# Second and third modulation vectors: products with the weight rows on TensorE, or weighed running sums on VectorE

## The reference, cut to what matters

```python
silu_c, silu_cc = jax.nn.silu(c), jax.nn.silu(c_ctx)
for i in range(2):                                    # first_block
    need_ctx = i < 1
    mod_lat = (silu_c @ w_ada[i] + b_ada[i])[:, None, :]
    mod_ctx = silu_cc @ w_ada[i] + b_ada[i]
    sh_a, sc_a, g_a, sh_m, sc_m, g_m = jnp.split(mod_lat, 6, axis=-1)
    h_lat = x * (1.0 + sc_a) + sh_a                   # and h_ctx with mod_ctx
    ...                                               # attention
    x = layer_norm(alpha * x + g_a * y_lat, ...)
    x = layer_norm(alpha * x + g_m * sq_relu_mlp(x * (1.0 + sc_m) + sh_m, mlp_w1[i], mlp_w2[i]), ...)
    ...                                               # the same for xc, only if need_ctx
mod = silu(c_2) @ ada_w_2[0] + ada_b_2[0]             # second_block: six more parts, used in the same way
```

## Time and profile before

| | us |
|---|---|
| median of three runs (lowest, highest) | 2645.05 (2643.78, 2648.04) |
| the profiled execution: its own time | 2641.13 |
| its span, first to last instruction | 2639.3 |
| PE busy | 2513.5 (95%) |
| DVE busy | 1460.6 (55%) |
| ACT busy | 1037.6 (39%) |
| POOL busy | 720.9 (27%) |

### The profile page before, as it was taken

One profiled execution on the slowest core, in us unless ns is written; L12 is line 12 of the kernel. 1 busy time (PEld: TensorE's weight loads), 2 busy tenths in 40 slices (PEclk: granted clock), 3 DMA queues, 4 the chain that ended last, 5 costly groups with the idle time before them and its releaser, 6 DMA issues.

```text
span 2639.3 us, 39599 instructions
## 1 busy us (share of the span) xinstructions
PE 2513.5 (95%) x16734; PEld 1439.8 (55%) x16734; DVE 1460.6 (55%) x2251; ACT 1037.6 (39%) x1665; POOL 720.9 (27%) x967
## 2 busy tenths in 40 slices
PE   6999998999999998999999999989999999999999
PEld 3566655555555576467654444745644445844444
DVE  4469865663332226688764433279977775633341
ACT  3457743333221114577643322243353224533230
POOL 0210000527878762310022000015454562011100
PEclk8999999999999999999999999999999999999999
DMA  6520013555542221210035543232212333333340
GB/s 242 177 79 18 2 65 128 165 171 200 181 155 93 84 81 51 81 36 18 18 109 176 179 144 112 74 104 68 89 58 78 104 120 103 84 86 96 109 147 32
DMA packets 205616, 271.43 MB, mean 103 GB/s; under 512 B 10047, under 2 KB 181438, under 8 KB 196222
## 3 DMA queue, kind: packets, MB, share of 16 engines
q1 hardware_dynamic: 199054, 247.05, 29.1%
q0 software_dynamic: 5280, 18.64, 2.0%
q10 hardware_dynamic: 1104, 3.21, 0.3%
HBM read 252.62 MB, written 10.49 MB: 100 GB/s over the span
## 4 chain that ended last, share of the span: by engine, by line
PE 75%; DVE 13%; ACT 6%; DMA 3%; issue 2%; SPq 1%; POOL 1%; DVEq 0%; POOLq 0%; ACTq 0%
PE PS L321 22%; PE PS L323 21%; PE PS L322 21%; PE PS L984 2%; PE PS L553 2%; DVE SM L1077 2%; DVE WB L300 2%; DVE AR L1083 1%; ACT WB L290 1%; DMA WS<-in_mlp_w 1%; ACT AR L1027 1%; DMA WS<-in_w_ada 1%; DVE X L1359 1%; DVE GT L1368 1%; DMA AR<-in_w_ada 1%
## 5 line engine op out<-in xcount | busy, mean ns | idle before, releaser
L321 PE MATMUL PS<-H,WB 128*128 128x512 bf16 (+1 forms) x1976 | 685.5, 347 | 19.7 <-DVE WB L300 9.1
L322 PE MATMUL PS<-H,WB 128*128 128x512 bf16 (+1 forms) x1976 | 684.4, 346 | 0.0
L323 PE MATMUL PS<-H,WB 128*128 128x512 bf16 (+1 forms) x1976 | 684.1, 346 | 0.0
L300 DVE TENSOR_TENSOR WB<-WS,WB 128x2048 bf16<-128x2048 f32 (+2 forms) x154 | 349.5, 2270 | 487.3 <-ACT WB L290 487.1
L290 ACT ACTIVATE WB<-WS 128x2048 bf16<-128x2048 f32 (+2 forms) x154 | 275.3, 1788 | 524.5 <-PE PS L323 291.7
L321 PE MATMUL PS<-AR,WB 128*128 128x512 bf16 (+1 forms) x1140 | 370.2, 325 | 5.4 <-DVE WB L300 4.5
L323 PE MATMUL PS<-AR,WB 128*128 128x512 bf16 (+1 forms) x1140 | 370.2, 325 | 0.0
L322 PE MATMUL PS<-AR,WB 128*128 128x512 bf16 (+1 forms) x1140 | 370.0, 325 | 0.0
L321 PEld LDWEIGHTS PS<-H,WB 128*128 128x128 bf16 x1976 | 194.2, 98 | 246.3 <-issue 55.1
L323 PEld LDWEIGHTS PS<-H,WB 128*128 128x128 bf16 x1976 | 194.4, 98 | 166.5 <-issue 3.5
L322 PEld LDWEIGHTS PS<-H,WB 128*128 128x128 bf16 x1976 | 194.4, 98 | 159.9 <-issue 6.6
(11 more groups left out here) (479 smaller groups left out, 4160.7 us busy)
## 6 DMA issues: line engine op xcount, KB each, us to landing
WS<-in_mlp_w SPq DMA_DIRECT2D x64, 1024.0 KB, 5.4
WS<-in_w_ada SPq DMA_DIRECT2D x40, 1024.0 KB, 5.0
WS<-in_w_in SPq DMA_DIRECT2D x26, 1024.0 KB, 5.3
WS<-in_ada_w SPq DMA_DIRECT2D x24, 1024.0 KB, 5.1
WS<-in_ffn_w_in SPq DMA_DIRECT2D x44, 512.0 KB, 5.1
WS<-in_ffn_w_out SPq DMA_DIRECT2D x10, 1024.0 KB, 5.0
AR<-in_w_ada SPq DMA_DIRECT2D x8, 1024.0 KB, 13.2
e_scratch<-EB POOLq DMA_DIRECT2D x16, 512.0 KB, 4.2
```

Source lines behind the costliest of these rows:

```text
L300: e.tensor_tensor(lo, staged_as(i, lo), hi, SUB).then_inc(dv.sem, dv.mark(("lo", i)))
L321: e.matmul(out_, l[0], r[0], start=start, stop=False)
L322: e.matmul(out_, l[0], r[1], start=False, stop=False)
L323: return e.matmul(out_, l[1], r[0], start=False, stop=stop)
```

## The change

The tiles of ada1 and ada2 are no longer multiplied on PE. Such a tile now has 512 rows and 512 columns (still 1 MB, 128 partitions x 4 x 512), and `weighed_dve` adds, for each of the four row blocks, the row times its SiLU value (a scalar per partition) to a running sum of 128 x 512 in ACC: four DVE instructions a tile, eight for the first group of ada1, where latent and context vector are both made. For i = 1 the context's other parts are left out. In the diff "ROUNDS" are such sums for 1024 columns (rounds 0 and 1, four tiles each) or 2048 columns (rounds 2 to 6, eight tiles each), 48 tiles in all as before. A round ends with one group of four matmuls by a matrix of ones (`summed_pe`), which adds up the 128 partitions of the four running sums, a copy by ACT, four transposes on PE and the bias on DVE. The slot of WS is free when DVE has done its last instruction on it.

The tiles also stand elsewhere: one after each dense tile in units 8 to 15 of ("w1", 0) (rounds 0 and 1), 16 in "w20" (rounds 2 and 3), 15 in units 1 to 15 of ("w1", 1), and 9 in "w21". ACC takes the place of ODD and its later users.

```diff
-            if home:
+            if home or whole == "weighed":
                 return i
...
                 if i >= NS:
-                    if tiles[i - NS][3]:
+                    if tiles[i - NS][3] == "weighed":
+                        dv.wait_ge(e, ("weighed tile", i - NS))
+                    elif tiles[i - NS][3]:
                         pe.wait_ge(e, ("w", i - NS))
...
+                if tiles[i][3] == "weighed":
+                    weighed_dve(e, i)
                 if tiles[i][3]:
                     continue
...
-                  ("w1", 0): ([("ada1", t) for t in range(24)] + [("ada2", t) for t in range(8)], 2, 4, "side"),
-                  ("w1", 1): ([("ada2", t) for t in range(8, 24)], 1, 2, "side")}
...
+            weighed_at("w20", ((2, 1), (2, 2), (2, 3), (2, 3), (3, 0), (3, 0), (3, 1), (3, 2))[t], 3, t)
+            weighed_at(("w1", 1), 2 * (1 + t), 4, t)
...
+        def weighed_dve(e, i):
+            r, t = round_of[i]
+            name, _, chunks, nv = ROUNDS[r]
...
+            at_w[i % NS].wait_ge(e, i)
+            if t < 2 and r:
+                pe.wait_ge(e, ("summed", r - 1))
+            for x in range(4):
+                k = 4 * (t % 2) + x
+                for v in range(nv):
+                    y, s = ACC[:, v * len(chunks) + t // 2, :], SIL[:, pair, k, v:v + 1]
+                    if k == 0:
+                        e.tensor_scalar(y, w[:, x, :], s, None, MUL)...
+                    else:
+                        dv.wait_ge(e, ("weighed", r, t // 2, v, k - 1))
+                        e.scalar_tensor_tensor(out=y, in0=w[:, x, :], scalar=s, in1=y, op0=MUL, op1=ADD)...
+        def summed_pe(e, r, ring):
+            bank(e, ring, ("summed", r))
+            dv.wait_ge(e, ("weighed", r))
+            for q in range(4):
+                m = e.matmul(ps(bank_of["summed", r], 512, slice(32 * q, 32 * q + 32)), mat["ones"][:, 0:32], ACC[:, q, :], start=True, stop=True)
+        def summed_act(e, r):
+            pe.wait_ge(e, ("summed", r), ("round turned", r - 1) if r else ("turned", "ada0", 2))
+            e.activation(MROWS, ps(bank_of["summed", r]), COPY)...
+        def round_turn_pe(e, r, ring):
+            bank(e, ring, ("round turned", r))
+            ac.wait_ge(e, ("summed rows", r))
+            for b in range(4):
+                m = e.transpose(at(("round turned", r), 128, b * 128), MROWS[:, b * 128:(b + 1) * 128], ident)
...
-                    dv.wait_ge(e, (f"ada{mod[0]}", "mods", 2))
+                    dv.wait_ge(e, (f"ada{mod[0]}", "mods", 2 * mod[1]))
...
-            if mod and tag != "wo0":
-                gains()
             for n, (u, f, s) in enumerate(groups(OUT[:3], segs)):
                 low_halves(e, through(tag, u, last))
                 gate(f, s)
                 beside_dve(e, tag, n)
+                if n == 2 and mod and tag != "wo0":
+                    gains()
```

More of the change, by code:

```diff
@@ L340, in sums @@
                     w, hi, lo = tile(e, (tag, i, c), src[k0 * 128:(k0 + nk) * 128, c0:c0 + nc_], nk, nc_, whole)
-                    if front and c == 0:
-                        front(e, i)
+                    if front:
+                        front(e, i, c)
                     for key, off, M in ms:
@@ L538, in build @@
         FIRST = [arena(6144 + t * 2048, 2048) for t in range(8)]
-        SETS = [(name, g) for name in ("ada0", "ada1", "ada2") for g in range(3)]
+        SETS = [("ada0", g) for g in range(3)]
         def ada_pe(e, name, t, ring="side"):
@@ L591, in first_mods_dve @@
             ada_dve(e, "ada0", 0)
-        BESIDE = {"wo0": ([("ada0", t) for t in range(16, 24)], 2, 4, "side5"),
-                  ("w1", 0): ([("ada1", t) for t in range(24)] + [("ada2", t) for t in range(8)], 2, 4, "side"),
-                  ("w1", 1): ([("ada2", t) for t in range(8, 24)], 1, 2, "side")}
+        BESIDE = {"wo0": ([("ada0", t) for t in range(16, 24)], 2, 4, "side5")}
         def beside_sum(stage, n):
@@ L606, in beside_sum, with weighed_at @@
             return ts[unit * per + r] if name and r < per else None, (name, t // 8) if r == per and t % 8 == 7 else None
+        ROUNDS = [("ada1", 0, (0, 1), 2), ("ada1", 0, (2, 3), 2)] + [(name, g, (0, 1, 2, 3), 1) for name, g in (("ada1", 1), ("ada1", 2), ("ada2", 0), ("ada2", 1), ("ada2", 2))]
+        WEIGHED, SUMMED, COPIED, TURNED = {}, {}, {}, {}
+        round_of = {}
+        def weighed_at(stage, n, r, *ts):
+            WEIGHED.setdefault((stage, n), []).extend((r, t) for t in ts)
@@ new lines, in build @@
+        for t in range(8):
+            weighed_at(("w1", 0), 4 * (8 + t), t // 4, t % 4)
+            weighed_at("w20", divmod(t, 4), 2, t)
+            weighed_at("w20", ((2, 1), (2, 2), (2, 3), (2, 3), (3, 0), (3, 0), (3, 1), (3, 2))[t], 3, t)
+            weighed_at(("w1", 1), 2 * (1 + t), 4, t)
+            weighed_at(*((("w1", 1), 2 * (9 + t)) if t < 7 else ("w21", (0, 0))), 5, t)
+            weighed_at("w21", divmod(3 + t, 4), 6, t)
+        for stage, r, summed, copied, turned in ((("w1", 0), 0, 46, 46, 47), ("w20", 1, (0, 0), 0, 2), ("w20", 2, (2, 1), 8, 10), ("wo1", 3, 0, 0, 1),
+                                                  (("w1", 1), 4, 17, 17, 18), ("w21", 5, (0, 2), 0, 1), ("w21", 6, (2, 3), 4, 5)):
+            SUMMED[stage, summed], COPIED[stage, copied], TURNED[stage, turned] = r, r, r
@@ new lines, in weighed_pe @@
+        def weighed_pe(e, stage, n):
+            for r, t in WEIGHED.get((stage, n), ()):
+                name, g, chunks, _ = ROUNDS[r]
+                c0 = g * 2048 + chunks[t // 2] * 512
+                round_of[tile(e, (stage, "weighed", r, t), mods[name][0][t % 2 * 512:t % 2 * 512 + 512, c0:c0 + 512], 4, 512, "weighed")] = r, t
+            if (stage, n) in SUMMED:
+                summed_pe(e, SUMMED[stage, n], "side" if stage[0] == "w1" else "dense")
+        def weighed_dve(e, i):
+            r, t = round_of[i]
+            name, _, chunks, nv = ROUNDS[r]
+            pair = mods[name][2]
+            w = staged(i).rearrange("p (k n) -> p k n", n=512)
+            at_w[i % NS].wait_ge(e, i)
[6 more added lines that the diff above has]
+                    if k == 0:
+                        e.tensor_scalar(y, w[:, x, :], s, None, MUL).then_inc(dv.sem, dv.mark(("weighed", r, t // 2, v, k)))
+                    else:
+                        dv.wait_ge(e, ("weighed", r, t // 2, v, k - 1))
+                        e.scalar_tensor_tensor(out=y, in0=w[:, x, :], scalar=s, in1=y, op0=MUL, op1=ADD).then_inc(dv.sem, dv.mark(("weighed", r, t // 2, v, k), ("weighed tile", i), ("weighed", r)))
@@ new lines, in round_turn_pe, with round_dve @@
+        def round_turn_pe(e, r, ring):
[3 more added lines that the diff above has]
+                m = e.transpose(at(("round turned", r), 128, b * 128), MROWS[:, b * 128:(b + 1) * 128], ident)
+            m.then_inc(pe.sem, pe.mark(("round turned", r)))
+        def round_dve(e, r):
+            name, g, chunks, nv = ROUNDS[r]
+            _, _, _, bias, dst = mods[name]
+            nc_, c0 = len(chunks), 16 * g + 4 * chunks[0]
+            pe.wait_ge(e, ("round turned", r))
+            dv.wait_ge(e, "biases")
+            for v in range(nv):
+                o = dst[:, c0:c0 + 4 * nc_, v].rearrange("p (j b) -> p j b", b=4)
+                x = at(("round turned", r), 512).rearrange("p (b j z) -> p j b z", b=4, z=32)[:, v * nc_:(v + 1) * nc_, :, 0]
+                y = bias[:, c0:c0 + 4 * nc_].rearrange("p (j b) -> p j b", b=4)
+                e.tensor_tensor(o, x, y, ADD).then_inc(dv.sem, dv.mark((name, "mods", g), ("free", ("round turned", r))))
@@ L613, in beside_pe @@
                 ada_turn_pe(e, *whole, BESIDE[stage][3])
+            weighed_pe(e, stage, n)
+            if (stage, n) in TURNED:
+                round_turn_pe(e, TURNED[stage, n], "side" if stage[0] == "w1" else "dense")
         def beside_act(e, stage, n):
@@ L618, in beside_act @@
                 ada_act(e, tile_[0], tile_[1] // 8)
+            if (stage, n) in COPIED:
+                summed_act(e, COPIED[stage, n])
         def beside_dve(e, stage, n):
@@ L1216, in then @@
                         two_tiles(i, n - 2 - (2 * i + 1) * ns)
-            linear(e, tag, src, OUT[:3], nks, rhs, segs, then, ring=ring)
+            linear(e, tag, src, OUT[:3], nks, rhs, segs, then, ring=ring, front=lambda e, i, c: weighed_pe(e, tag, (i, c)))
             c0, nc_, ms = OUT[3]
@@ L2292, in build @@
         CTR, CTI = [4, 5], [6, 7]
-        SETS5 = [ST, [ODD[:, i, :] for i in range(4)]]
+        SETS5 = [ST, [ACC[:, i, :] for i in range(4)]]
         S5B, S5M = ST[0], [ST[1][:, 0:256], ST[1][:, 256:512], ST[2][:, 0:256], ST[2][:, 256:512]]
```

11 lines of the change are left out of this document (8 added, 3 removed).

## The result

The changed kernel takes 2629.8 us (median of five executions, 2624.4 to 2636.6), the kernel before 2643.8 beside it: a ratio of 0.9944 with an interval of 0.9929 to 0.9959. It is faster by 0.6%, but 25 us slower than the 2605 predicted, 8 above the upper end of the range. Timed once more it took 2634.9, a ratio of 0.9953 (0.9940 to 0.9967).

A forecast was written before the change was run, and what follows sets the result against it. PE was taken to bound all four changed stages: its work falls 47.8 us, less waits of 5.7, 1.5 and 1.0, is 39.6, so 2605 us from 2645.05; 8-in-10 range 2596 to 2622.

The forecast's parts named there:

- What leaves PE, 58.5 us, and what comes, 10.7: On PE, 48 whole tiles at 1.10 us and six turns leave; seven groups and turns come; work falls by 47.8 us.
- What a weighed tile costs DVE: On DVE, 3.4 us a tile with one vector, 6.0 at most with two; DVE keeps up.
- Rival 3: Rounds 0 to 3: GpSimd and DVE exclude each other, weighed instructions take 1.76 us; 2655 us, 6%.
- The loop of the weights: WS slot's load, high half, low half: 10.0 us against 10.35; waits of 1.5 us in ("w1", 1), 1 in "w21".
- rival 2: The weights' loop bounds ("w1", 1) and "w21": 11.9 us, 1.5 over 10.35 a tile, 30 us in all; 2632 us, 12%.
- The double in "w20", 5.7 us: End of unit 2 of "w20": late dense load delays ACT's copy of round 2; PE waits 5.7 us at the turn.
- The sum: Whole kernel: 47.8 - 5.7 - 1.5 - 1.0 = 39.6 us less, so a median of 2605 us.
- The step that failed: All four changed stages: PE is busy nearly throughout, so what leaves it shortens the kernel if weights still arrive.
- 48 x 0.33: PE's time for a unit of ("w1", 0) without its two whole tiles, given as 15.6 us.
- the waits at none: Lower end of the forecast's own case, 2598 to 2616 us, which has 75%.
- the two terms named for the upper end: Upper end, 2616 us: each of 23 loops 0.4 over, and the double's load at 7.6; put at 13 us more.
- two groups and two turns: Sign of being right: "w20" longer by some 6 us plus two groups and three turns.

The follow-up runs named there:

- the experiment on the whole tile's price: The kernel before, with matmuls of six of each eight whole tiles of the second and third modulation 64 columns wide, not 512: 2618.8 us, ratio 0.9900.
- the fourth experiment: The changed kernel with the weighed tiles of rounds 0 to 3 placed earlier (the earlier placement), part sums still in the tables' buffer: 2626.9 us, ratio 0.9933.
- 32 columns: The changed kernel with each weighed operation that adds to a running sum 32 columns wide in place of 512: 2608.3 us, ratio 0.9862.
- short tables: The changed kernel with the last three of GpSimd's sixteen tables only cleared and stored, not built: 2610.9 us, ratio 0.9874.
- the fifth experiment: The changed kernel with rounds 0 to 3 placed earlier, "w20" part sums in ACC, not EB, and round 3's turn at sum 11 of "w20": 2606.1 us.

## Why the prediction was wrong

- **What leaves PE, 58.5 us, and what comes, 10.7.** Right. ("w1", 0) and ("w1", 1) lost 38.4 and 14.4 where the terms give 38.5 and 15.4, and the experiment on the whole tile's price bears out 1.1 us.
- **What a weighed tile costs DVE.** Right in size and right that DVE keeps up: 806 ns an operation for 750 to 870. Rival 3 took the exclusion of DVE and GpSimd as a delay of DVE that decides from 1.04 us. In the stretch where GpSimd is busiest beside them (560 to 720) they took 0.85, as forecast.
- **The loop of the weights.** Right: no wait of 1.5 us a tile in ("w1", 1) or "w21"; rival 2's 30 us did not come. That its time, 2632, lies near the 2629.8 is chance. "w21" took 0.7 more than its terms.
- **The double in "w20", 5.7 us.** Right in place, cause and nearly size: 6.3, 5.4 when run again. ACT's high half waits for its load and the copy L669 runs behind it:

```profile
911.87 1.91 ACT L292 ACTIVATE WB<-WS 128x2048 bf16<-128x2048 f32 x1 [32.23 <-DMA WS<-in_mlp_w]
913.69 0.58 ACT L669 ACTIVATE STAT<-PS 128x512 f32<-128x512 f32 x1
```

  Removing it alone was worth nothing that the medians can tell, as the fourth experiment shows: without it PE waits longer at the tail. The sum has nothing for the slower clock behind this wait, some 2 us.
- **The step that failed** is the first one: "PE sets the time of all four stages, and what leaves PE shortens the kernel, as long as the weights still arrive". It asks of the weights alone what would be late next. Something else had a due time in "w20": a chain on GpSimd that starts when DVE has its angles, runs for 400 us beside both stages, and must be over before ACT's copy at the end. I asked of GpSimd only whether it slows DVE. The trace of before had both numbers, the last store at 976.59 and the copy at 996.60. With 38 us taken from the work ahead of the tail and the tables' pace unchanged (401.7 us from 556.4, so the last store at 958), PE at 974 would still not have waited; the kernel with 32 columns, which stores it at 960.9, has no wait. So it took both: PE sooner, and the tables 27 us longer. The first was on my page; the second follows from the very rule that I weighed, read in the other direction.
- Without this wait the kernel is 3 to 6 us above the sum's 2605: 2610.9 with short tables and 2608.3 with 32 columns, both with the wait at the turn that the sum contains. The 2606.1 of the fifth experiment are nearer to it by luck: that kernel has no wait at the turn, for which the sum has 5.7.
- Slips in the working, none of which decides: 48 x 0.33 is 15.8 and not 15.6, and in the timeline of after the wide matmuls start 0.215 apart and the others 0.109, which gives the 15.6; the waits at none give 2597 as the lower end and not 2598, and the two terms named for the upper end add up to 11.6 and not 13, while 2616 is 11 above 2605; "w20" has two groups and two turns, and the third turn, that of round 3, stands with its group in "wo1".

## What to carry to other kernels

When a stage gets shorter, list each wait of its end that costs nothing now (the semaphore waits in the code, not those in the profile) and read for each how long before it the awaited thing was done; whatever has less to spare than the stage gains is the next bound. A chain on an idle-looking engine (GpSimd was busy for 29% of the span) belongs on this list, with the pace that it will have beside the new work and not the one it has now. Where two users share a buffer across such a chain, another buffer may be worth more than the whole change: here 19.5 us for moving 768 columns, once the earlier placement had made room in ACC, where the change itself had brought 14.
